# An encoder block: a projection that opens with three weight lists in step instead of two, and a convolution split by even and odd time steps

## The reference, cut to what matters

```python
h = layer_norm(x, in_ln_g, in_ln_b)                 # (2048, 1024)
proj = h @ w_in                                     # 1792 columns: q 512, k 128, v 128, a 512, gate 512
u = a * sigmoid(gate)                               # (2048, 512)
conv[t] = sum_{k<31} w[k] * u[t - 30 + k] + b       # per channel, zero before t = 0
```

## Time and profile before

| what | value |
|---|---|
| time, median of 3 runs (lowest, highest) | 1985.78 us (1984.66, 1986.21) |
| the profiled execution: its own time | 1987.32 us |
| span of the core in it | 1985.5 us |
| mean granted TensorE clock | 0.976 of full speed |
| `phase_project` within the span | from 0 to about 370 us |
| last matmul of L545 starts | 363.89 us |
| first instruction of `phase_rest` on DVE | 370.51 us |

### The profile page before, as it was taken

The page is one execution under the profiler, slowest core; times in us unless marked ns, Lnnn a source line. Parts: engine busy times, 40 slices in busy tenths (PEclk is TensorE's granted clock), DMA queues, the critical chain, the costliest instruction groups (busy, mean ns, idle before and its releaser), DMA issues.

```text
span 1985.5 us, 27468 instructions
## 1 busy us (share of the span) xinstructions
PE 1866.0 (94%) x8520; PEld 1527.0 (77%) x8520; DVE 1572.7 (79%) x1878; ACT 973.6 (49%) x1504; POOL 971.9 (49%) x694
## 2 busy tenths in 40 slices
PE   3899999479999889999999899999999899999998
PEld 3788888367777668888888678888888788888886
DVE  8779879379999878888888888888888755866687
ACT  4555455277777644444444544444444433233453
POOL 5477797336667344444445554454444566630000
PEclk8999999789999989999999999999999999999999
DMA  7411201544456242222322332223223644487553
...
DMA packets 200718, 258.55 MB, mean 130 GB/s; under 512 B 12240, under 2 KB 131536, under 8 KB 200144
## 3 DMA queue, kind: packets, MB, share of 16 engines
...
## 4 chain that ended last, share of the span: by engine, by line
PE 59%; DVE 11%; ACT 5%; issue 4%; DMA 1%; POOL 1%; SPq 1%; ACTq 0%; DVEq 0%; POOLq 0%
PE u_mm L2027 38%; PE d_y L2422 20%; ACT m_ce L1510 1%; DVE u_forms L1647 1%; ACT m_tps L1502 1%; DVE m_stat L1836 1%; DVE m_top L1867 1%; DVE m_den L1880 1%; DVE u_w_lo L1638 1%; PE m_y L2075 1%; ACT m_probT L1537 1%; DVE m_cc L1829 1%; ACT u_forms L1345 0%; DVE m_mix_lo L1909 0%; DVE m_tps L1905 0%
## 5 line engine op out<-in xcount | busy, mean ns | idle before, releaser
L2027 PE MATMUL u_mm<-u_forms,u_w_hi 128*128 128x512 f32 x2464 | 768.1, 393 | 28.0 <-issue 15.4
L2027 PEld LDWEIGHTS u_mm<-u_forms,u_w_hi 128*128 128x128 f32 x2464 | 466.4, 190 | 129.0 <-issue 27.4
L2027 PE MATMUL u_mm<-u_forms,u_w_lo 128*128 128x512 f32 x1232 | 483.5, 392 | 0.0
L2422 PE MATMUL d_y<-d_wd,d_a_hi 128*128 128x512 f32 x1232 | 381.0, 391 | 5.9 <-DVE d_a_lo L894 3.9
L2422 PEld LDWEIGHTS d_y<-d_wd,d_a_hi 128*128 128x128 f32 x1232 | 232.0, 189 | 54.7 <-DVE d_a_lo L894 4.3
L2027 PEld LDWEIGHTS u_mm<-u_forms,u_w_lo 128*128 128x128 f32 x1232 | 233.7, 190 | 49.1
L2422 PE MATMUL d_y<-d_wd,d_a_lo 128*128 128x512 f32 x616 | 240.5, 390 | 0.0
L1678 DVE SCALAR_TENSOR_TENSOR u_y<-u_z,u_taps,u_y 128x1024 f32<-128x1024 f32 x176 | 222.6, 1287 | 15.1 <-DVE u_z L1692 3.5
L524 DVE SCALAR_TENSOR_TENSOR a_acc<-a_glu,a_taps,a_acc 128x2048 f32<-128x2048 f32 x84 | 197.8, 2355 | 15.2 <-DVE a_acc L524 14.4
L1157 POOL TENSOR_TENSOR u_w_sum<-u_w_raw 128x512 f32<-128x512 f32 x44 | 56.9, 1293 | 299.9 <-DMA u_w_raw<-w_up 299.9
L545 PE MATMUL a_mm<-a_hT_hi,a_w_hi 128*128 128x512 f32 (+1 forms) x448 | 176.7, 394 | 0.0
...
## 6 DMA issues: line engine op xcount, KB each, us to landing
u_w_raw<-w_up SPq DMA_DIRECT2D x44, 1024.0 KB, 4.8
...
gated_scr<-u_s SPq DMA_DIRECT2D x88, 256.0 KB, 2.0
d_wd_raw<-w_down SPq DMA_DIRECT2D x88, 256.0 KB, 5.2
gated_scr<-u_gy SPq DMA_DIRECT2D x44, 256.0 KB, 2.1
u_stage<-h1T_scr SPq DMA_DIRECT2D x9, 1024.0 KB, 5.7
...
```

Source lines behind the costliest of these rows:

```text
L2027: last = nc.tensor.matmul(mm[BANK[s]][:], w[:, s, k, :], forms[:, POS[s], part, k, :], start=(s in FRESH and k == 0 and w is w_hi and part ...
L2422: m = nc.tensor.matmul(dy[u % BANKS][:], a[:, u % 2, k, :], wd[:, ph % 2, k, part, :], start=(k == 0 and a is a_hi and part == HI_PART), s ...
```

## The change

The list order becomes a 0, gate 0, q 0, a 1, gate 1, q 1, a 2, gate 2, a 3, gate 3, q 2 to q 5. The first three run in step in the opening, 24 steps of depth to a block: `AHEAD` says how many of them stand before each of the four transposes of the next block, and the rest stands behind the last transpose. The other 11 run one by one.

In the opening, rows wait in `h_rows`, which lies in the space of the last block of `hT_hi`; the last block's rows stay in `xs`. DVE adds b for block 0 itself (`shift`), behind each `scale`; POOL, which no longer does that, starts with the low parts of the first three lists. For blocks 1 to 3 POOL still adds b. On ACT, `hi_of` of block 0 is placed between the three `weights_hi`; from block 1 on, `take_gate` stands ahead of `hi_of(n, 3)`, and all four `norm` of the next block behind it. The loops over blocks are written out.

The convolution is computed for even and odd steps apart. `glu` holds a tile's even and odd phases in two halves. With E the sum of the 16 even taps over one phase, O that of the 15 odd taps over the other, and M the sum over both phases added together with neighbouring taps added together, the even result is E + O and the odd one M - O - E. DVE makes E and M over 1024 steps each, in turn, so that an operation waits for the last but one; ACT and POOL make O over 1025 steps in two pieces. The last tile's store stands behind list q 4.

```diff
-ACT_TAPS = 9
+LEAD = HALO // 2
+ETAPS, OTAPS = LEAD + 1, LEAD
+FOLD = SEQ // 2
+REACH = LEAD + FOLD
+PIECES = ((0, FOLD // 2), (FOLD // 2, FOLD // 2 + 1))
+NP = len(PIECES)
...
 
-STREAM = [("a", 0), ("gate", 0)]
-for _j in range(1, CT):
-    STREAM += [("a", _j), ("gate", _j), ("qkv", _j - 1)]
-STREAM += [("qkv", _j) for _j in range(CT - 1, QT)]
+STREAM = [("a", 0), ("gate", 0), ("qkv", 0), ("a", 1), ("gate", 1), ("qkv", 1), ("a", 2), ("gate", 2), ("a", 3), ("gate", 3)]
+STREAM += [("qkv", _j) for _j in range(2, QT)]
+OPEN = 3
 IN_TILES = [{"a": QT, "gate": QT + CT, "qkv": 0}[_kind] + _j for _kind, _j in STREAM]
...
+        with ExitStack() as early:
+            early.enter_context(nc.sbuf_tensor("a_first_blocks", [P, NB - 1, KT, BLK], F32))
+            h_rows = early.enter_context(nc.sbuf_tensor("a_h_rows", [P, RB, D], F32))
+        hT_hi = sb("a_hT_hi", [P, NB, KT, BLK], F32R)
+        hT_lo = sb("a_hT_lo", [P, NB, KT, BLK], F32R)
...
+        with ExitStack() as early:
+            early.enter_context(nc.sbuf_tensor("a_glu_first", [P, 2, REACH + 1], F32))
+            w3_hi = early.enter_context(nc.sbuf_tensor("a_w3_hi", [P, KT, P], F32R))
+            w3_lo = early.enter_context(nc.sbuf_tensor("a_w3_lo", [P, KT, P], F32R))
+        glu = sb("a_glu", [P, 2, 2, REACH + 1])
+        sig = sb("a_sig", [P, 2, BLK // 2])
...
-        spare = sb("a_spare", [P, D])
+        spare = sb("a_spare", [P, D + 2])
...
+        prod = spare[:, :].rearrange("p (s t) -> p s t", s=2)
         conv_out = xs[:, :, :].rearrange("p (s a) d -> p s (a d)", s=2)
...
+        part, both = gb[:, 0:FOLD + 1], gb[:, REACH + 1:REACH + 1 + REACH]
         ident = sb("a_ident", [P, P])
...
+            for i in range(OPEN, OPEN + 2):
+                sp.wait_ge(wlo_ok, i - OPEN + 1)
+                load_list(i)
...
+            weights_hi(0)
+            hi_of(0, 0)
+            weights_hi(1)
+            hi_of(0, 1)
+            weights_hi(2)
+            hi_of(0, 2)
+            hi_of(0, 3)
+            block_root(1)
+            for r in range(RB):
+                norm(1, r)
+            for n in range(1, NB):
+                last, e = n == NB - 1, OPEN * (n - 1)
+                if n == 1:
+                    take_a(e, 0, n - 1, 1)
                 hi_of(n, 0)
+                if n > 1:
+                    take_a(e, 0, n - 1, 1)
                 hi_of(n, 1)
-                if not first:
-                    take_a(2 * n - 2, 0, n * BLK + (HALO - BLK), 2)
                 if not last:
                     block_root(n + 1)
                 hi_of(n, 2)
-                if not last:
-                    norm(n + 1, 0)
+                take_gate(e + 1, n - 1, 2)
                 hi_of(n, 3)
...
                         norm(n + 1, r)
-                if not first:
-                    take_gate(2 * n - 1, n - 1, 3)
-
-            block(0, True, False)
-            for f in range(ROT // 2):
-                act.dma_start(pos[f * NT:(f + 1) * NT, :], positions.rearrange("o (t q) -> (o t) q", t=NT)).then_inc(pos_ld, 16)
-            act.dma_start(freq[:], con[:, CON_FREQ:CON_FREQ + 4]).then_inc(pos_ld, 16)
...
+                take_q(e + 2, n - 1, 3)
+                store_q(e + 2, n - 1)
+                if n == 1:
+                    for f in range(ROT // 2):
+                        act.dma_start(pos[f * NT:(f + 1) * NT, :], positions.rearrange("o (t q) -> (o t) q", t=NT)).then_inc(pos_ld, 16)
+                    act.dma_start(freq[:], con[:, CON_FREQ:CON_FREQ + 4]).then_inc(pos_ld, 16)
+            e = OPEN * (NB - 1)
+            take_a(e, 0, NB - 1, 1)
+            weights_hi(3)
+            take_gate(e + 1, NB - 1, 2)
+            weights_hi(4)
+            take_q(e + 2, NB - 1, 3)
+            store_q(e + 2, NB - 1)
...
 
             pool.sem_inc(part_ok, 2)
             pool.wait_ge(par_ld, 64)
-            for r in range(RB):
-                add_bias(0, r)
-            weights_lo(0, 0)
-            weights_lo(1, 1)
+            for i in range(OPEN):
+                weights_lo(i)
             add_bias(1, 0)
             add_bias(1, 1)
-            with pool.Fori(1, NB - 1) as n:
+            for n in range(1, NB):
                 add_bias(n, 2)
                 add_bias(n, 3)
-                add_bias(n + 1, 0)
-                add_bias(n + 1, 1)
-                gate(2 * n - 1, 0, n * BLK + (HALO - BLK))
-            add_bias(NB - 1, 2)
...
+            def shift(r):
+                dve.wait_ge(scaled_ok, r + 1)
+                nc.vector.tensor_tensor(row(0, r), row(0, r), b_bc, ALU.add).then_inc(h_ok, 1)
+
+            for r in range(3):
+                scale(0, r)
+                shift(r)
+            lo_of(0, 0)
+            scale(0, 3)
+            shift(3)
+            lo_of(0, 1)
+            stats(1, 0)
+            lo_of(0, 2)
+            stats(1, 1)
+            lo_of(0, 3)
+            stats(1, 2)
+            stats(1, 3)
+            block_stats(1)
+            scale(1, 0)
+            scale(1, 1)
+            for n in range(1, NB):
+                scale(n, 2)
+                scale(n, 3)
+                lo_of(n, 0)
+                if n < NB - 1:
+                    stats(n + 1, 0)
+                    stats(n + 1, 1)
+                lo_of(n, 1)
+                if n < NB - 1:
+                    stats(n + 1, 2)
+                    stats(n + 1, 3)
+                    block_stats(n + 1)
+                lo_of(n, 2)
+                if n < NB - 1:
+                    scale(n + 1, 0)
...
+                chain.inc(nc.vector.tensor_tensor(both, phase(0, 0, REACH), phase(1, 0, REACH), ALU.add))
+                chain.inc(nc.vector.tensor_scalar(even, phase(0, 0, FOLD), tap_of(j, 0), cbias[:, bass.ds(j, 1)], ALU.mult, ALU.add))
+                chain.wait(1)
+                chain.inc(nc.vector.tensor_scalar(mixed, both[:, 0:FOLD], flat(ctaps[:, bass.ds(j, 1), 0:1]), cbias2[:, bass.ds(j, 1)],
+                                                  ALU.mult, ALU.add))
+                for k in range(1, ETAPS):
+                    chain.wait(chain.n - 1)
+                    chain.inc(nc.vector.scalar_tensor_tensor(out=even, in0=phase(0, k, FOLD), scalar=tap_of(j, 2 * k), in1=even,
+                                                             op0=ALU.mult, op1=ALU.add))
+                    chain.wait(chain.n - 1)
+                    chain.inc(nc.vector.scalar_tensor_tensor(out=mixed, in0=both[:, k:k + FOLD], scalar=flat(ctaps[:, bass.ds(j, 1), k:k + 1]),
+                                                             in1=mixed, op0=ALU.mult, op1=ALU.add))
+                to = conv_out[:, bass.ds(j % 2, 1), :].rearrange("p o (m f) -> p f (o m)", f=2)
+                dve.wait_ge(part_ok, (OTAPS - 1) * NP * (j + 1) + 2)
+                dve.wait_ge(conv_free, 16 * (j + 1))
+                chain.wait(chain.n - 1)
+                chain.inc(nc.vector.tensor_tensor(to[:, 0, :], even, part[:, 0:FOLD], ALU.add))
+                chain.wait(chain.n - 1)
+                chain.inc(nc.vector.tensor_tensor(to[:, 1, :], mixed, part[:, 1:], ALU.subtract))
                 chain.wait()
-                dve.wait_ge(part_ok, (ACT_TAPS - 1) * NB * (j + 1) + 2)
-                dve.wait_ge(conv_free, 16 * (j + 1))
-                nc.vector.tensor_tensor(conv_out[:, bass.ds(j % 2, 1), :].rearrange("p o t -> p (o t)"), acc[:], part,
-                                        ALU.add).then_inc(conv_ok, 1)
+                assert chain.n == OPS
+                nc.vector.tensor_tensor(to[:, 1, :], to[:, 1, :], even, ALU.subtract).then_inc(conv_ok, 1)
...
-            def products(slot, ks, rhs_at, bank, done):
...
+            def product(hi, lo, n, k, bank):
+                for w, h in ((hi, hT_hi), (hi, hT_lo), (lo, hT_hi)):
+                    last = nc.tensor.matmul(mm[bank][:], w[:, k, :], h[:, n, k, :], start=(k == 0 and w is hi and h is hT_hi),
+                                            stop=(k == KT - 1 and w is lo))
+                return last
+
+            def sweeps(n, first, last):
+
+                for at in range(first, last):
+                    i, k = divmod(at, KT)
+                    if at == 0:
+                        pe.wait_ge(lo_ok, RB * (n + 1))
+                    if k == 0:
+                        if n == 0:
+                            pe.wait_ge(wlo_ok, i + 1)
+                        else:
+                            pe.wait_ge(mm_free, OPEN * (n - 1) + i + 1)
+                    m = product(list_hi(i), list_lo(i), n, k, 1 + i)
+                    if k == KT - 1:
+                        m.then_inc(mm_ok, 1)
+
+            ALL = OPEN * KT
+            AHEAD = {1: (10, 15, 18, 21), 2: (6, 12, 18, 21), 3: (6, 12, 18, 21)}
             pe.wait_ge(con_ld, 16)
...
+            for n in range(1, NB):
+                done = 0
                 for r in range(RB):
-                    pe.wait_ge(lo_ok, RB * n + (r - 1))
+                    sweeps(n - 1, done, AHEAD[n][r])
```

(67 more changed lines are left out.)

232 lines of the change are left out of this document (96 added, 136 removed).

## The result

The changed kernel takes 1991.24 us (median of 9 runs, 1988.48 to 1993.76), the kernel before 1985.78 us beside it (9 runs). The medians differ by 5.5 us. The ratio is 1.0024, 95% interval [1.0015, 1.0033]: slower by 0.24%, 4.8 us. Forecast were 1989.2 us, 3.4 us more than before, within 1982.0 to 1994.5. In the profiled execution after (1992.52 us, span 1990.7) the opening ends at T = 130.9 (PE's end, 370.14 + 0.23, less 239.5), where 130.4 was forecast.

A forecast was written before the change was run, and what follows sets the result against it. PE was taken as the bound, with waits in the opening and the convolution hidden. PE's end +5.7 us, less 2.3 for the earlier last store, gave +3.4 on the median 1985.78: 1989.2 us, range 1982 to 1994.5.

The forecast's parts named there:

- The account: Whole phase: 11 lists, 239.5 us, follow the opening, so PE ends at T + 239.5; T 130.4, PE 5.7 us later.
- break-even of 124.7: End of the opening at which PE would finish as before, 21.8 us later than the old opening's end.
- the cases that the prediction called slower: Whole time above 1989.8 us, chance 0.45, beside the same at 0.45 and faster, below 1981.8, at 0.10.
- a lump of 1.0 us: Opening: added to T, 129.4 to 130.4, because the same walk over the old order gave 101.8 against 102.9.
- rival 2: Behind the opening: POOL's tap sums use up 2 us of cover and delay list q 4's weights; 1993 us, chance 0.17.
- Block 0: Opening's start: DVE's added shifts and contention with POOL's low parts delay the next block's scale to 42.3, 7.8 us lost.
- Block 1: Opening: ACT's gate work ahead of norm costs 2.5 us; PE stands 6.7 us, until 66.1.
- Blocks 2 and 3: Opening: too few steps behind the last transposes, a 3.35 us gap; slow clock about 1.9 us behind each gap.
- The stream: Single lists behind the opening: PE must not stall; cost 0, with 2 us of cover for POOL's weights.
- The convolution: DVE's part falls from 59 to 46 us a tile, 13 us saved four times, all hidden, worth nothing to PE.
- The end: Phase's end: last tile's store goes out a list earlier; 2.3 us gained, bounds 0 and 3.4.
- Rival 1: Opening: the third list fills PE's waits, T 113.4, 1972 us; chance 0.13 with all partial forms.

The follow-up runs named there:

- Experiments 1 to 4: Single edits of the changed kernel: POOL adds block 0's shift, 0.9999; norm ahead of gate, 0.9987; more depth behind the last transposes, 1.0008; low parts later, 0.9996.
- Experiment 2: Changed kernel with ACT normalising the next block's first row before hi_of(n, 3) and take_gate after all its rows; ratio to before 0.9987.
- kernel 9: Changed kernel with the old two-list opening, including POOL's additions and the whole old order of ACT; new convolution and early last store kept; ratio to before 0.9999.
- kernel 7: Changed kernel with POOL's three low parts waiting for block 0's four shifted rows and ACT's norm ahead of take_gate; ratio to before 0.9968.
- kernel 8: kernel 7 with, in addition, a depth table leaving 6 to 8 steps behind the last transposes; ratio to before 0.9960.
- 10: Changed kernel with POOL adding block 0's shifts again ahead of the low parts, and ACT's norm ahead of take_gate; ratio to before 0.9967.
- 12: kernel 7 with the shift's parameter row b moved 48 bytes further on in its buffer; ratio to before 0.9970.
- kernel 5: Changed kernel with the last tile's 1 MB store put back behind the last qkv list; ratio to before 1.0036.

## Why the prediction was right, step by step

- **The account.** T was forecast at 130.4 and is 130.9, against a break-even of 124.7. Start moved by 4.0 us, which is 130.9 - 124.7 less the 2.25 of the store. Experiments 1 to 4 move T and start alike, within 0.1 us. The measured time lies among the cases that the prediction called slower (above 1989.8, chance 0.45), and 2 us above its one number. That T came out within 0.5 us is in part luck: block 0 came 0.5 us early, the stretch from block 1's first product to block 2's took 1.0 us more than its terms, and a lump of 1.0 us, put on top for what an earlier walk had missed, covered it. Two of the sums are also off as written: block 3's start, from 91.0 with its terms, is 112.7 and not 113.1, and in rival 2 58 sums at 0.05 us more are 2.9 us and not 2.6.
- **Block 0.** Forecast were transposes at 16.9, the end of `lo_of(0, 3)` at 36.5, the next `scale` at 42.3; the trace has 16.89, 36.04 and 41.83. The low parts held DVE 2.2, 2.0 and 1.0 us, 5.2 in all (forecast 2, 2 and 0.9). Had each held DVE for its full 2.33 us, as the prediction worked out from the Trainium skill (page "SBUF — State Buffer", section "Who interferes with whom"), it would be 7.0. The page makes the shared ports an exclusive lock, and the trace fits that: each of the three operations of DVE came when a low part had already begun, and waited for its rest. POOL's three took 6.01 us for two and 3.33 for the third in place of 2.33 each, as if they waited for DVE in turn. `shift` starts 0.03 us behind the end of its `scale`, not 0.18; four times 0.15 is about the 0.5 us of difference. The reading that DVE's 3.02 us before was a wait for POOL's addition rests on this line of the kernel before, which ends at 21.39, with the earlier trace rows:

```profile
15.61 5.78 POOL L372 TENSOR_TENSOR a_glu<-a_glu,a_gb 128x1024 f32<-128x1024 f32 x2 [14.71 <-DVE a_glu L457]
```

- **Block 1.** Forecast: `norm` done at 63.8, PE idle 6.7 us until 66.1. Measured: the `scale` behind it at 63.80, 6.27 until 66.21. Experiment 2 shows that ACT's order puts 2.5 of the 6.3 us there, the 2.5 that the prediction named; the other 3.8 stay without it.
- **Blocks 2 and 3.** The gap was 2.94 us (forecast 3.35), block 2 began at 92.16 (91.0). From block 1's first product it took 25.95 us where the terms gave 24.9. The mis-sized term is the clock: behind the 6.27 us gap PE's first 14 products took 6.01 us (66.21 to 72.22), where full speed gives 3.2, so the slow clock cost 2.8 us and not 1.9. Behind the 2.94 us gap it cost 1.7. The 1.0 us laid on top at the end was a lump for such things, and it hid this.
- **The stream.** No stall. POOL's cover was underestimated: list q 4's low part was ready at 317.3 for its start at T + 9 lists = 326.9, 9.6 us of cover and not 2:

```profile
314.86 2.40 POOL L424 TENSOR_TENSOR a_w_lo<-a_w_raw,a_w_hi 128x1024 fp32r<-128x1024 f32 x1
```

The sums took 1.20 us, not 1.25, and the gates 1.11. With 58 sums and 8 gates that is about 4 of the 7.6 us; the rest was not taken apart. Rival 2 was far away.
- **The convolution** freed DVE, whose last result comes at 341.0 (339.74 + 1.23), 29 us ahead of PE's end (forecast 22). Its worth to PE was nothing, as forecast: PE never paused behind T, with the old convolution or the new (kernel 9).
- **The end.** 2.25 us gained, forecast 2.3.
- **Rival 1** (the third list fills the waits, T 113.4) did not come, but kernel 7 reaches T 118.2 with two edits, and kernels 7, 8, 10 and 12 are 0.3 to 0.4% faster than before. The third list was not the fault; what fed it was.

The sum said +3.4 us. Start moved by 4.0. The ratio gives 4.8 us and the medians 5.5; the difference to 4.0 lies within what `phase_rest` scatters, and no run takes it apart.

## What to carry to other kernels

Moving an operation to an engine that is free on average can put it beside another engine's operation with the same needs; one wait that keeps them apart brought PE's end 6.7 us forward here with no work removed. When PE is given more work to fill waits, look at what feeds it next: the order of another engine's small steps (ACT's norm behind the gate) cost 7.0 us, 4.0 of them as longer waits and most of the rest through the slow clock behind those. And hold lists of work that lie behind the bound (here the convolution) at zero until they are seen to end a wait.

## What the runs showed that had not been expected

- POOL's addition of 128x1024 took 2.00 us with rows in `a_glu` and 2.35 to 2.40 with rows in `a_q_out`, `a_spare`, `a_h_rows` or `a_xs`. Moving b by 48 bytes didn't alter it (2.37 with rows in `a_h_rows`). What decides is open.
- The granted clock behind a gap of PE: behind 6.3 us the first product took 0.79 us. Behind 2.94 us it took 0.51 in the changed kernel and 0.80 in kernel 5, and the clock was low in both (0.57 and 0.60 of full from 92 to 96 us). Behind 3.76 us both kinds occurred too (0.50 in kernel 2, 0.79 in kernel 7). The same length can go either way: behind 2.81 us in kernel 9 the transposes ran fast (1.09 us for eight) and the products stayed 0.23 us apart, behind 2.79 us in kernel 8 the products were 0.43 us apart from 59.73 on. Behind 1.47 us and less it stayed full. A first product at full speed is thus no sign that the gap was free.
